# A two-layer hybrid network: one unused product in front of long runs of matrix products, and one loop turn written out on TensorE

## The chip, the cores and the metric

The kernel runs on one core of a Trainium2 chip (trn2). The metric is the time of one execution on the device, in microseconds (us). Every weight of the network comes from the chip's memory once; activations stay in the core's SBUF.

## The reference

One sequence of 256 tokens, width 1024, fp32, goes through two blocks.

```python
# first block: i = 0, 1
h = rms_norm(x, norm_mix_g[i])
x = x + (dsa_mixer(h, ...) if i == 0 else retention_mixer(h, ...))
x = x + conv_ffn(rms_norm(x, norm_ffn_g[i]), f_w_up[i], f_conv_w[i], f_conv_b[i], f_w_down[i])
# second block
h = rmsnorm(x, norm_mix_w) * (1 + scale_m) + shift_m
x = x + gate_m * hybrid_mixer(h, ...)
h = rmsnorm(x, norm_mlp_w) * (1 + scale_f) + shift_f
x = x + gate_f * (square(relu(h @ w_up)) @ w_down)
return rmsnorm(x, norm_final_w)
```

`dsa_mixer` is attention over a latent of 128 with an index that selects 64 keys; `retention_mixer` has 4 heads; `conv_ffn` projects 1024 to 2 x 2816, convolves over 3 tokens, gates by silu and projects back; `hybrid_mixer` joins a state-space scan (4 groups of 8 heads) and a pooling branch by gates. `c` enters by `silu(c) @ w_ada` as scale, shift and gate.

## The kernel before, in words

**Slabs.** All weights come as 381 slabs of 128 x 1024 fp32 (512 KB), in the order in which they are used, through a ring of six slots (`RING`). A slab holds eight 128x128 tiles. Numbers of the first slab of each stage are `S_AIN` (0), `S_AOUT`, `S_FFN0`, `S_B`, `S_BOUT`, `S_FFN1`, `S_DT`, `S_GRP`, `S_GATE`, `S_MERGE`, `S_WOUT`, `S_MLP`.

**The split multiplication.** TensorE multiplies in the format fp32r, and accuracy is kept by splitting both operands in two. ScalarE writes `w_hi` (L187, `split_hi`, a rounding copy), VectorE writes `w_lo = w_raw - w_hi` (L192, `split_lo`), and each tile then takes three products, `mm3`, lines L200 to L202: w_hi with the high part of the activation, w_hi with its low part, w_lo with its high part. The first operand of `pe.matmul` behind the output is the stationary one (128 weights columns), the second is the moving one, here 256 columns, the tokens. A profile row `ps<-a_hi,w_hi` is such a product; PEld rows are the loads of the stationary operand. `slab_gemm` does the eight tiles of one slab, 24 products, into one PSUM bank; `down_slab` uses one slab for eight output tiles, also 24 products; `two_slabs` takes two slabs tile by tile at the start of a stage, while the activation's tiles still arrive (`each(k)` waits for tile k). `both_slab` streams the high and low part of an activation as one moving operand of 512 columns (`L232`) with w_lo in another (`L233`).

**Operands in SBUF.** `w_raw`, `w_hi`, `w_lo` (6 x 4096 bytes per partition each) lie one behind the other, then a strip of 64 bytes, `between`, then `a_hi`, `a_lo`, `b_both` (tiles of 256 fp32, high and low), then `c_both`, whose tiles are 258 columns wide. So a tile of a_hi, a_lo or b_both begins 64 bytes past a multiple of 512 from any tile of weights, and the tiles of c_both begin at changing remainders.

**The order.** It is written out by hand for each engine and kept by semaphores: `w_lo_ready` counts split slabs (TensorE waits for it in `slab_ready`), `w_used` counts slabs that TensorE has finished, and frees the slot. TensorE goes through the stages `attention_pe`, `ffn_pe` (L = 0), `retention_pe`, `ffn_pe` (L = 1), `ssd_pe` and the last feed-forward.

- `ffn_pe` works on 22 pairs of up-slabs; the down-slab of pair p follows the up-slabs of pair p + 2. After the first pairs a hardware loop runs `LATER` = 4 turns of `UNROLL` = 4 pairs, on TensorE, ScalarE and VectorE alike; its semaphore values are computed from the turn (`val`). In the first feed-forward the slabs before the loop are 0 and 1 (two_slabs), 2 (`up_half(1, 0)`), a sum of squares, 3 (`up_half(1, 1)`), the pair 2 and `down(0)`; in the second they are `up_half(0, 0)`, a sum of squares (L264), `up_half(0, 1)` and so on.
- `retention_pe` has 12 slabs for each head j = 0 to 11, of which 4 to 7 (`v_slab`) have the activation as the stationary operand and 512 weights columns moving; `weigh` (L1246 to L1248) comes behind slab 8 and `sums` (L1252) behind slab 10. Head 0 is written out, heads 1 to 3 are a loop. `out_pe` is the output projection, m = 0 to 7, two slabs each here.
- `ssd_pe` works on four groups of 12 slabs (the small transposes L1588 and L1591 stand in it), `pools` (moving operand c_both), 16 gate slabs, the merge and `out_pe` with one slab for each m. Its `keep_going` is 24 unused products.

Row names in the profile: L1246 is a product of `weigh`, L1359 and L1374 are VectorE's lines in the retention heads (the decayed scores, and the low part of the heads' result, which is the operand of the output projection).

## Time and profile before

| | |
|---|---|
| median of three runs | 1194.18 us (1191.48 to 1194.28) |
| the profiled execution | 1193.18 us |
| its span, first to last instruction | 1191.4 us |
| mean granted TensorE clock | 0.998 |
| instructions | 25489, of them 9030 products on TensorE |
| busy: ScalarE | 712.9 us (60%) |
| bytes read from the chip's memory | 233.73 MB, 197 GB/s over the span |

The profile is one execution. Its page gives busy shares of the engines (PE is TensorE, DVE VectorE, ACT ScalarE), the chain of work that ended last, and groups of instructions by line. Products are pipelined: each is booked with its whole length, and the next starts before it ends, so the step between two products is not the length that a row shows. It has to be taken from starts: of single products in the timeline, or of the first and last product of a line in a stretch, with their number. "Idle" rows name what released an engine. Times in the timeline are microseconds from the span's start.

### The profile page before, as it was taken

To read this page: it belongs to the slowest core of one execution; us is meant where nothing else is said; L and a number is where in the kernel's file an instruction comes from. 1 tells how busy PE (TensorE), PEld (TensorE's weight loads), DVE (VectorE), ACT (ScalarE), POOL (GpSimd) and SP (SyncE) were. 2 spreads that over 40 slices of the span, in tenths; PEclk is the share of its full clock that TensorE was granted. 3 is DMA by queue.
4 is the path that set the end of the run, shared out by engine and by line. 5 is a ranking of instruction groups with operands and counts; after the bars stand their busy time and mean duration, and the time that the engine had idled before them with its cause. 6 is when DMAs were issued, how large, how long until landed. Compare 5 with 4: busy or idle time off the path is not lost.

```text
span 1191.4 us, 25489 instructions
## 1 busy us (share of the span) xinstructions
PE 1168.6 (98%) x9030; PEld 1114.1 (94%) x9030; DVE 976.2 (82%) x1775; ACT 712.9 (60%) x1111; POOL 33.3 (3%) x62
## 2 busy tenths in 40 slices
PE   9999999999999999999999999999999999999997
PEld 7989999999899999999999999999899899999996
DVE  7877998888998898899888799998996667666666
ACT  6577655556546456565555577877866456544553
POOL 0000000000000010000000000000000000000000
PEclk9999999999999999999999999999999999999999
DMA  7634676664766786756656436458545555655550
GB/s 279 188 114 165 207 238 227 223 221 151 242 235 229 265 295 230 251 193 232 224 198 192 161 112 244 148 188 184 169 159 196 187 185 211 200 189 186 184 176 36
DMA packets 72752, 235.71 MB, mean 198 GB/s; under 512 B 7392, under 2 KB 16096, under 8 KB 72560
## 3 DMA queue, kind: packets, MB, share of 16 engines
q1 hardware_dynamic: 64016, 203.86, 51.2%
q0 software_dynamic: 8528, 30.98, 7.6%
q8 instruction: 41, 0.67, 0.2%
q14 instruction: 23, 0.19, 0.1%
q10 hardware_dynamic: 144, 0.02, 0.0%
HBM read 233.73 MB, written 1.09 MB: 197 GB/s over the span
## 4 chain that ended last, share of the span: by engine, by line
PE 83%; DVE 9%; ACT 4%; issue 3%; DMA 0%; DVEq 0%; SPq 0%; ACTq 0%
PE ps L200 25%; PE ps L201 24%; PE ps L202 24%; PE ps L232 3%; DVE w_lo L192 3%; PE ps L233 2%; DVE arena L1937 1%; ACT w_hi L187 1%; PE ps L1602 1%; DMA w_raw<-stream 0%; ACT arena L756 0%; DVE arena L1925 0%; DVE arena L453 0%; PE ps L1236 0%; PE ps L1246 0%
## 5 line engine op out<-in xcount | busy, mean ns | idle before, releaser
L200 PE MATMUL ps<-a_hi,w_hi 128*128 128x256 f32 x1656 | 468.0, 283 | 2.4 <-DVE w_lo L192 1.6
L192 DVE TENSOR_TENSOR w_lo<-w_raw,w_hi 128x1024 fp32r<-128x1024 f32 x381 | 461.1, 1218 | 10.6 <-ACT w_hi L187 4.8
L201 PE MATMUL ps<-a_lo,w_hi 128*128 128x256 f32 x1656 | 462.2, 279 | 0.0
L202 PE MATMUL ps<-a_hi,w_lo 128*128 128x256 f32 x1656 | 461.9, 279 | 0.0
L187 ACT ACTIVATE w_hi<-w_raw 128x1024 fp32r<-128x1024 f32 x381 | 390.6, 1048 | 23.3 <-PE ps L202 17.9
L200 PEld LDWEIGHTS ps<-a_hi,w_hi 128*128 128x128 f32 x1656 | 310.9, 188 | 7.9 <-issue 3.8
L201 PEld LDWEIGHTS ps<-a_lo,w_hi 128*128 128x128 f32 x1656 | 310.6, 188 | 0.5
L202 PEld LDWEIGHTS ps<-a_hi,w_lo 128*128 128x128 f32 x1656 | 310.7, 188 | 0.2 <-issue 0.2
L200 PE MATMUL ps<-b_both,w_hi 128*128 128x256 f32 x560 | 158.1, 282 | 4.2 <-DVE b_both L927 3.5
L201 PE MATMUL ps<-b_both,w_hi 128*128 128x256 f32 x560 | 156.4, 279 | 0.0
L202 PE MATMUL ps<-b_both,w_lo 128*128 128x256 f32 x560 | 156.3, 279 | 0.0
L200 PEld LDWEIGHTS ps<-b_both,w_hi 128*128 128x128 f32 x560 | 105.1, 188 | 6.4 <-DVE b_both L927 4.7
L201 PEld LDWEIGHTS ps<-b_both,w_hi 128*128 128x128 f32 x560 | 105.1, 188 | 0.0
L202 PEld LDWEIGHTS ps<-b_both,w_lo 128*128 128x128 f32 x560 | 105.0, 188 | 0.0
L1026 ACT ACTIVATE arena<-arena,par 128x256 f32<-128x256 f32 x88 | 52.7, 601 | 74.5 <-DVE arena L1087 74.5
L201 PE MATMUL ps<-c_both,w_hi 128*128 128x258 f32 (+1 forms) x280 | 79.5, 284 | 0.0
L200 PE MATMUL ps<-c_both,w_hi 128*128 128x258 f32 (+1 forms) x280 | 79.0, 282 | 0.0
L202 PE MATMUL ps<-c_both,w_lo 128*128 128x258 f32 (+1 forms) x280 | 78.8, 281 | 0.0
L2171 ACT ACTIVATE arena<-arena 128x256 f32<-128x256 f32 x32 | 16.4, 512 | 82.8 <-DVE arena L2222 82.8
L1037 ACT ACTIVATE b_both<-arena 128x256 fp32r<-128x256 f32 x44 | 18.4, 419 | 71.8 <-DVE arena L1101 71.8
L453 DVE CUSTOM_DVE_ANT_0 arena<-arena 128x1024 f32<-128x1024 f32 x48 | 58.5, 1219 | 1.3 <-DMA arena<-ada 1.1
L1087 DVE TENSOR_TENSOR arena<-ps,inv 128x256 f32<-128x256 f32 x88 | 36.9, 421 | 23.6 <-PE ps L202 23.5
(309 smaller groups left out, 1665.5 us busy)
## 6 DMA issues: line engine op xcount, KB each, us to landing
w_raw<-stream SPq DMA_DIRECT2D x381, 512.0 KB, 3.8
arena<-ada POOLq DMA_DIRECT2D x48, 512.0 KB, 5.3
c_both<-cum_rows POOLq DMA_DIRECT2D x4, 1024.0 KB
arena<-x SPq DMA_DIRECT2D x2, 512.0 KB, 4.5
con<-consts SPq DMA_DIRECT2D x1, 1024.0 KB, 5.8
arena<-row_cols POOLq DMA_DIRECT2D x2, 512.0 KB
out<-arena SPq DMA_DIRECT2D x4, 256.0 KB, 2.2
arena<-c_rows POOLq DMA_DIRECT2D x1, 512.0 KB, 4.2
```

The source lines that it names most:

```text
L187: act.activation(w_hi[:, s % RING], w_raw[:, s % RING], ACT.Copy).then_inc(w_hi_ready, 1)
L192: dve.tensor_tensor(w_lo[:, s % RING], w_raw[:, s % RING], w_hi[:, s % RING].bitcast(F32), ALU.subtract).then_inc(w_lo_ready, 1)
L200: pe.matmul(o, wh, xh, start=start, stop=False, skip_group_check=shared)
L201: pe.matmul(o, wh, xl, start=False, stop=False, skip_group_check=shared)
L202: return pe.matmul(o, wl, xh, start=False, stop=stop, skip_group_check=shared)
L232: pe.matmul(ps[:, bank, :].rearrange("p (i t) -> p i t", i=2), w_hi[:, s % RING, t], both[:, k], start=first and k == 0, stop=False)
L233: mm = pe.matmul(ps[:, bank, 0:SEQ], w_lo[:, s % RING, t], both[:, k, 0], start=False, stop=last and k == NT - 1)
L453: dve.tensor_tensor_reduce(ada_raw[:, DOT_BUF[i]], ada_raw[:, DOT_BUF[i]], cond_row, 1.0, 0.0, ALU.mult, ALU.add, o).then_inc(dot_done, 1)
L1026: act.activation(conv[:, p % 2, half], up[:, p % 2, half], ACT.Identity, bias=prm(p, 6 + half, it), scale=prm(p, 3 * half + 2, it)).then_i ...
L1037: act.activation(b_hi[:, p % 4], glu[:, p % 2], ACT.Copy).then_inc(f["hi"], 1)
L1087: dve.tensor_tensor(up[:, p % 2, half], ps[:, 6 - 2 * (p % 2) + half, 0:SEQ], inv[:, :], ALU.mult).then_inc(f["up_out"], 1)
L2171: act.activation(relu[:, n % 3], up_m[:, n % 3], ACT.Relu, bias=up_shift[:, n % 3:n % 3 + 1]).then_inc(relu_ready, 1)
```

## The change

A new helper, `settle`, issues one product at the beginning of a run: stationary operand the first tile of w_hi in the ring slot of the coming slab, moving operand the first 256 columns of w_lo in the same slot, into the PSUM bank that the run is about to fill. Its result is not used, since the first real product of the run starts the accumulation anew. The two operands lie exactly `RING * SLAB` elements (24576 bytes) apart, the "zero distance" of the change's name: both begin at the same remainder of 4096. `slab_gemm`, `two_slabs` and the helpers above them get a flag `lead` that asks for it, behind the wait for the slab and, where tiles are awaited one by one, behind the wait for the first tile. It is set for attention slabs 0 and 4; in the first feed-forward for the two first slabs, slab 3 and the first slab of the loop's first turn; in each retention head for slabs 9 and 11, and for the two first slabs of head 0; in the second feed-forward for its second slab; for gate slab 3; and in both `out_pe` for m = 1.

So that the loop of the first feed-forward has it once and not in each turn, its first turn is written out in front of it on TensorE, and its loop there starts at turn 1. The other engines' programs are unchanged.

```diff
--- before.py
+++ after.py
@@ -201,22 +201,32 @@
             pe.matmul(o, wh, xl, start=False, stop=False, skip_group_check=shared)
             return pe.matmul(o, wl, xh, start=False, stop=stop, skip_group_check=shared)
 
-        def slab_gemm(pe, s, o, hi, lo, it=None, ds=0, first=True, last=True, each=None):
+        def settle(pe, s, o):
+
+            pe.matmul(o, w_hi[:, s % RING, 0:P], w_lo[:, s % RING, 0:SEQ], start=True, stop=True)
+
+        def slab_gemm(pe, s, o, hi, lo, it=None, ds=0, first=True, last=True, each=None, lead=False):
 
             slab_ready(pe, s, it, ds)
+            if lead and each is None:
+                settle(pe, s, o)
             for k in range(NT):
                 if each:
                     each(k)
+                    if lead and k == 0:
+                        settle(pe, s, o)
                 t = slice(k * P, (k + 1) * P)
                 mm = mm3(pe, o, w_hi[:, s % RING, t], w_lo[:, s % RING, t], hi[:, k], lo[:, k],
                          first and k == 0, last and k == NT - 1)
             mm.then_inc(w_used, 1)
 
-        def two_slabs(pe, s, outs, hi, lo, each):
+        def two_slabs(pe, s, outs, hi, lo, each, lead=False):
 
             slab_ready(pe, s + 1)
             for k in range(NT):
                 each(k)
+                if lead and k == 0:
+                    settle(pe, s, outs[0])
                 t = slice(k * P, (k + 1) * P)
                 for i, o in enumerate(outs):
                     n = (s + i) % RING
@@ -401,10 +411,10 @@
                     pe.wait_ge(taken, base + m - 3)
                 o = ps[:, 4 + (m + 2) % 4, 0:SEQ]
                 if two:
-                    slab_gemm(pe, s0 + 2 * m, o, hi, lo, last=False, each=None if m else each[0])
+                    slab_gemm(pe, s0 + 2 * m, o, hi, lo, last=False, each=None if m else each[0], lead=m == 1)
                     slab_gemm(pe, s0 + 2 * m + 1, o, hi[:, NT:2 * NT], lo[:, NT:2 * NT], first=False, each=None if m else each[1])
                 else:
-                    slab_gemm(pe, s0 + m, o, hi, lo, each=None if m else each[0])
+                    slab_gemm(pe, s0 + m, o, hi, lo, each=None if m else each[0], lead=m == 1)
 
         def out_act(act, s0, per, v, g):
             load_root_table(act, v)
@@ -524,8 +534,8 @@
             def operand(k):
                 pe.wait_ge(a_ready, k + 1)
 
-            def in_slab(n, each=None):
-                slab_gemm(pe, n, ps[:, in_bank(n), 0:SEQ], a_hi, a_lo, each=each)
+            def in_slab(n, each=None, lead=False):
+                slab_gemm(pe, n, ps[:, in_bank(n), 0:SEQ], a_hi, a_lo, each=each, lead=lead)
 
             def key_sums(n):
                 pe.wait_ge(key_sq, n + 1)
@@ -569,7 +579,7 @@
                                    ki_dup[r, 0:w], start=True, stop=True)
                 mm.then_inc(idx_ready, 1)
 
-            in_slab(0, operand)
+            in_slab(0, operand, lead=True)
             in_slab(1)
             in_slab(2)
             in_slab(3)
@@ -578,7 +588,7 @@
             pe.wait_ge(res_ready, NT)
             key_sums(0)
             key_sums(1)
-            in_slab(4)
+            in_slab(4, lead=True)
             in_slab(5)
             pe.wait_ge(key_diag, 1)
             pe.matmul(ps[:, 7, :], ones, diag[:, :, :].rearrange("p b t -> p (b t)"), start=True, stop=True).then_inc(key_spread, 1)
@@ -974,16 +984,16 @@
 
         def ffn_pe(pe, L, s0, v):
 
-            def up_half(p, half, it=None, each=None):
+            def up_half(p, half, it=None, each=None, lead=False):
 
                 if p >= 2:
                     pe.wait_ge(f["up_out"], val(2 * FF_PAIRS * L + 2 * (p - 2) + half + 1, it, 2 * UNROLL))
-                slab_gemm(pe, pair_at(s0, p) + half, ps[:, 6 - 2 * (p % 2) + half, 0:SEQ], a_hi, a_lo, it, 3 * UNROLL, each=each)
-
-            def up_pair(p, it=None):
+                slab_gemm(pe, pair_at(s0, p) + half, ps[:, 6 - 2 * (p % 2) + half, 0:SEQ], a_hi, a_lo, it, 3 * UNROLL, each=each, lead=lead)
+
+            def up_pair(p, it=None, lead=False):
 
                 for half in range(2):
-                    up_half(p, half, it)
+                    up_half(p, half, it, lead=lead and not half)
 
             def down(p, it=None):
                 pe.wait_ge(f["operand"], val(FF_PAIRS * L + p + 1, it, UNROLL))
@@ -992,17 +1002,21 @@
             if L:
                 up_half(0, 0, each=ready(a_ready, NT * v)(pe))
                 sum_added(pe, v)
-                up_half(0, 1)
+                up_half(0, 1, lead=True)
                 up_half(1, 0)
             else:
-                two_slabs(pe, s0, [ps[:, 6 + half, 0:SEQ] for half in range(2)], a_hi, a_lo, ready(a_ready, NT * v)(pe))
+                two_slabs(pe, s0, [ps[:, 6 + half, 0:SEQ] for half in range(2)], a_hi, a_lo, ready(a_ready, NT * v)(pe), lead=True)
                 up_half(1, 0)
                 sum_added(pe, v)
-            up_half(1, 1)
+            up_half(1, 1, lead=not L)
             pe.wait_ge(inv_ready, v)
             up_pair(2)
             down(0)
-            with pe.Fori(0, LATER) as it:
+            if not L:
+                for u in range(UNROLL):
+                    up_pair(3 + u, lead=u == 0)
+                    down(1 + u)
+            with pe.Fori(0 if L else 1, LATER) as it:
                 for u in range(UNROLL):
                     up_pair(3 + u, it)
                     down(1 + u, it)
@@ -1261,9 +1275,9 @@
                     if 4 <= j < 8:
                         v_slab(own, j - 4, it)
                     elif h == 0 and j == 0:
-                        two_slabs(pe, own, [ps[:, i, 0:SEQ] for i in range(2)], a_hi, a_lo, ready(a_ready, 2 * NT)(pe))
+                        two_slabs(pe, own, [ps[:, i, 0:SEQ] for i in range(2)], a_hi, a_lo, ready(a_ready, 2 * NT)(pe), lead=True)
                     elif h or j > 1:
-                        slab_gemm(pe, own, ps[:, j % 4, 0:SEQ], a_hi, a_lo, it, HEAD)
+                        slab_gemm(pe, own, ps[:, j % 4, 0:SEQ], a_hi, a_lo, it, HEAD, lead=j in (9, 11))
                     if h == 0 and j == 2:
                         sum_added(pe, 2)
                     if h == 0 and j == 3:
@@ -1660,7 +1674,7 @@
                     pe.wait_ge(u_done, 2 * GROUPS)
                 else:
                     pe.wait_ge(gate_ready, m - 3)
-                slab_gemm(pe, gate_at(m), ps[:, m % 4, 0:SEQ], a_hi, a_lo)
+                slab_gemm(pe, gate_at(m), ps[:, m % 4, 0:SEQ], a_hi, a_lo, lead=m == 3)
                 if m == 2:
                     tail_sums(GROUPS - 1, None)
 
```

TensorE in the first feed-forward, from the last product of `down(0)` into the loop, before (names as in the profile: output, then operands; L200 to L202 are the split multiplication, `ISA` and branch rows belong to the loop, `ffn_up_out` counts VectorE's evictions of the up-slabs):

```order
L202 MATMUL ps<-b_both,w_lo 128x256
L1005 UNCONDITIONAL_BRANCH
L1005 ISA
L196 ISA [waits ffn_up_out]
L200 MATMUL ps<-a_hi,w_hi 128x256 [waits w_lo_ready]
L201 MATMUL ps<-a_lo,w_hi 128x256
L202 MATMUL ps<-a_hi,w_lo 128x256
```

The same place after, where the written-out turn now begins,

```order
L202 MATMUL ps<-b_both,w_lo 128x256
L206 MATMUL ps<-w_lo,w_hi 128x256 [waits w_lo_ready,ffn_up_out]
L200 MATMUL ps<-a_hi,w_hi 128x256
L201 MATMUL ps<-a_lo,w_hi 128x256
L202 MATMUL ps<-a_hi,w_lo 128x256
```

and the entrance of its loop, one turn later:

```order
L202 MATMUL ps<-b_both,w_lo 128x256
L1019 UNCONDITIONAL_BRANCH
L1019 ISA
L196 ISA [waits ffn_up_out]
L200 MATMUL ps<-a_hi,w_hi 128x256 [waits w_lo_ready]
```

What moved: the lead (L206) now carries the two waits of the turn's first slab, and the entrance of the loop, with its branch, stands 12 slabs (288 products) further back.

TensorE in the second feed-forward, from the last product of `up_half(0, 0)` over the sum of squares (L264) to `up_half(0, 1)`, before:

```order
L202 MATMUL ps<-a_hi,w_lo 128x256
L264 MATMUL ps<-sq,con 128x256 [waits sq_added]
L200 MATMUL ps<-a_hi,w_hi 128x256 [waits w_lo_ready]
L201 MATMUL ps<-a_lo,w_hi 128x256
L202 MATMUL ps<-a_hi,w_lo 128x256
```

and after, where the sum is at L274:

```order
L202 MATMUL ps<-a_hi,w_lo 128x256
L274 MATMUL ps<-sq,con 128x256 [waits sq_added]
L206 MATMUL ps<-w_lo,w_hi 128x256 [waits w_lo_ready]
L200 MATMUL ps<-a_hi,w_hi 128x256
L201 MATMUL ps<-a_lo,w_hi 128x256
L202 MATMUL ps<-a_hi,w_lo 128x256
```

What moved: one product stands between the sum and the slab, and has taken over the wait for w_lo; nothing else in this feed-forward differs.

## Rows read from the trace of the kernel before

**Rows 1.** The page's first part: busy time and share of the span.
```profile
PE 1168.6 (98%) x9030; PEld 1114.1 (94%) x9030; DVE 976.2 (82%) x1775; ACT 712.9 (60%) x1111; POOL 33.3 (3%) x62
```

**Rows 2.** The page's chain that ended last, by line.
```profile
PE ps L200 25%; PE ps L201 24%; PE ps L202 24%; PE ps L232 3%; DVE w_lo L192 3%; PE ps L233 2%; DVE arena L1937 1%; ACT w_hi L187 1%; PE ps L1602 1%; DMA w_raw<-stream 0%; ACT arena L756 0%; DVE arena L1925 0%; DVE arena L453 0%; PE ps L1236 0%; PE ps L1246 0%
```

**Rows 3.** Line L202: count, min/median/max ns, first and last start, in three stretches.
```profile
L202 PE MATMUL ps<-a_hi,w_lo x343: 279/279/279, 498.8 to 673.3; 128*128 128x256 f32 x172
L202 PE MATMUL ps<-b_both,w_lo x176: 279/279/279, 512.6 to 681.8; 128*128 128x256 f32 x176
...
L202 PE MATMUL ps<-a_hi,w_lo x304: 279/279/279, 125.8 to 283.8; 128*128 128x256 f32 x152
L202 PE MATMUL ps<-b_both,w_lo x166: 279/279/279, 131.5 to 291.6; 128*128 128x256 f32 x166
...
L202 PE MATMUL ps<-b_both,w_lo x113: 278/280/280, 455.3 to 494.8; 128*128 128x256 f32 x113
```

**Rows 4.** The same view of L202 in three other stretches.
```profile
L202 PE MATMUL ps<-a_hi,w_lo x31: 276/276/276, 43.4 to 53.6; 128*128 128x256 f32 x31
...
L202 PE MATMUL ps<-a_hi,w_lo x23: 276/276/276, 104.8 to 112.3; 128*128 128x256 f32 x23
...
L202 PE MATMUL ps<-a_hi,w_lo x32: 276/276/276, 898.8 to 909.3; 128*128 128x256 f32 x32
```

**Rows 5.** Timeline of TensorE (start, length) at three starts, and L202 behind two.
```profile
125.50 0.39 PE L200 MATMUL ps<-a_hi,w_hi 128*128 128x256 f32 x1 [0.82 <-DVE w_lo L192]
125.73 0.28 PE L201 MATMUL ps<-a_lo,w_hi 128*128 128x256 f32 x1
...
757.73 0.37 PE L200 MATMUL ps<-a_hi,w_hi 128*128 128x256 f32 x1
757.93 0.28 PE L201 MATMUL ps<-a_lo,w_hi 128*128 128x256 f32 x1
...
L202 PE MATMUL ps<-a_hi,w_lo x17: 276/276/276, 758.0 to 763.5; 128*128 128x256 f32 x17
...
717.97 0.36 PE L200 MATMUL ps<-a_hi,w_hi 128*128 128x256 f32 x1
718.17 0.28 PE L201 MATMUL ps<-a_lo,w_hi 128*128 128x256 f32 x1
...
L202 PE MATMUL ps<-a_hi,w_lo x16: 279/279/279, 718.3 to 723.6; 128*128 128x256 f32 x16
```

**Rows 6.** Timeline of TensorE in the pool projection, moving operand c_both.
```profile
895.94 0.29 PE L202 MATMUL ps<-c_both,w_lo 128*128 128x256 f32 x1
896.07 0.28 PE L200 MATMUL ps<-c_both,w_hi 128*128 128x256 f32 x1
896.18 0.29 PE L201 MATMUL ps<-c_both,w_hi 128*128 128x256 f32 x1
896.31 0.29 PE L202 MATMUL ps<-c_both,w_lo 128*128 128x256 f32 x1
```

**Rows 7.** Timeline of VectorE and TensorE around three slabs of the first feed-forward.
```profile
124.23 1.22 DVE L192 TENSOR_TENSOR w_lo<-w_raw,w_hi 128x1024 fp32r<-128x1024 f32 x1
...
132.56 1.22 DVE L192 TENSOR_TENSOR w_lo<-w_raw,w_hi 128x1024 fp32r<-128x1024 f32 x1
...
134.09 0.28 PE L200 MATMUL ps<-a_hi,w_hi 128*128 128x256 f32 x1
```

**Rows 8.** Waits of TensorE from 300 to 455 us: total, times, longest.
```profile
PE ps L1246 <- DVE arena L1359: 0.7, 1, 0.7
PE ps L200 <- DVE b_both L1374: 0.7, 2, 0.5
```

**Rows 9.** Windows: length, busy us of PE, PEld, DVE, ACT, POOL, clock, DMA.
```profile
44.00:53.00 9.00, 9.00 (x81) 9.00 (x81) 8.75 (x33) 5.40 (x10) 0.00 (x0) 1.00 0.52 154
...
140.00:180.00 40.00, 40.00 (x342) 40.00 (x341) 37.25 (x63) 25.42 (x38) 1.59 (x3) 1.00 0.71 233
```

**Rows 10.** The page's costliest groups: VectorE's split of a slab.
```profile
L192 DVE TENSOR_TENSOR w_lo<-w_raw,w_hi 128x1024 fp32r<-128x1024 f32 x381 | 461.1, 1218 | 10.6 <-ACT w_hi L187 4.8
```

## Prediction

> **What bounds the kernel now.** I read the page first. TensorE is busy in 98% of the span, VectorE in 82% [rows 1], and in the chain that ended last lines L200 to L202, the three products of the split multiplication, hold 73% [rows 2]. So time is made of products multiplied by the step from one product to the next. "Busy" says nothing of that step, because a product is booked with 279 ns while the next one starts long before it ends. I therefore asked for line L202 in long stretches: the row gives the number of its products and the start of the first and the last one, and there is one L202 product in every three.
>
> In the second feed-forward 343 + 176 = 519 of them start between 498.8 and 681.8 us [rows 3]: 183.0 us over 518 steps is 353.3 ns for three products, **117.8 ns for one**. In the first feed-forward's loop 304 + 166 = 470 start between 125.8 and 291.6 us: 353.5 ns, again 117.8; the output projection of the retention (113 from 455.3 to 494.8 us) gives 352.7. But there are runs of the same instruction and shapes, at the same granted clock of 1.00, the 2.4 GHz level [rows 9], that go faster: 31 from 43.4 to 53.6 us, 340 ns for three; 23 from 104.8 to 112.3 us, 341; 32 from 898.8 to 909.3 us, 339 [rows 4]. That is **113.3 ns for one**. The booked time differs too, 276 against 279 or 280 ns, so a row shows at a glance which pace its stretch had. Within a stretch minimum, median and maximum are equal or nearly so: a run keeps the pace it began with, across slabs, across the loop's turns and from a_hi to b_both as moving operand. The pace is a property of how the run started.
>
> What decides it the rows don't tell outright. Two runs behind the very same code, the two small transposes of L1591 in two groups of the state-space part, have the same 0.20 us between their first two products; one then goes on with products of 276 ns, the other with 279 [rows 5]. After the wait that ends at 125.50 us (first to second product 125.73 - 125.50 = 0.23 us) the long loop began slow and stayed slow for all its slabs. Where the moving operand's place relative to the weights' changes from product to product (the tiles of c_both lie 258 columns apart, those of a_hi 256), the step wanders: 0.13, 0.11, 0.13 us in a row [rows 6], and right behind it stands the 113 ns stretch of 898.8 us. So the relative place of the two operands acts on the step, and a run can be pushed from one pace into the other. That is what the change tries: one product whose two operands lie a whole number of slabs apart, w_lo against w_hi of the same ring slot, put at the start of a run.
>
> **The change, part by part.** (1) Leads: 14 places, two of them in the loop over heads that turns three times, so 12 + 6 = 18 executed. Each is one 128x256 product; I cost it at one step, 0.118 us: 18 x 0.118 = 2.1 us on the path, since TensorE is the path nearly everywhere. Bounds: nothing, where it stands in a gap that ends with another engine's work; 0.23 us, the first step after a wait [rows 5]: 4.1 us for all. I take the 2.1, nearest to the rows of running products.
>
> (2) The runs behind them, in slabs of 24 products. First feed-forward from the unrolled turn on: 59 slabs. Second, from its second slab: 65. Output projection of the retention from its third slab: 14. Heads: slabs 9 and 10 four times, 8; slab 11 with the next head's first four, 3 x 5, and the last slab 11: 16. Attention slabs 4 and 5: 2. Gates 3 to 11: 9. Output of the state-space part, tiles 1 to 7: 7. Together 180 slabs, 4320 products. If each goes from 117.8 to 113.3 ns that is 4320 x 4.5 ns = **19.4 us**. Bounds of this term: nothing (no run changes pace) and the full 4.5 ns; below nothing if the lead pushes a run to a slower step (third rival). I take the full 4.5, because only two steady paces occur on this pair of operands, a run holds what it has, and a product at another distance is the one thing that I see precede a change of pace.
>
> (3) Runs that bring nothing. Up-slab 3, pair 2 and the first down-slab of the first feed-forward (113 us on) end in a wait for VectorE's w_lo, which ended at 125.45 us (124.23 + 1.22) [rows 7]: whatever TensorE saves there it waits longer; zero. The first four slabs of the attention could give 96 x 4.5 = 0.4 us; their successors are short sums that also wait for others; zero, with 0.4 kept for the range. The two places with two slabs at once are fast already.
>
> (4) The retention heads. From the heads to the output projection TensorE waits for two results of VectorE, three times, 1.4 us together [rows 8], and a faster TensorE asks for them earlier. Of the gain on the heads' 24 slabs, 24 x 24 x 4.5 ns = 2.6 us, I take off 1.0. Their 512-column products step otherwise and I count nothing for them.
>
> (5) Unrolling the first turn on TensorE: 288 more products are written out, none more is executed, and the loop starts at turn 1 for the first feed-forward. The semaphore values are the same. The output projection at 455 us is written out too and has the loop's pace [rows 3], so I cost this at zero; the cover would be gone if the instruction stream were not there in time, which would show as a gap at the loop's entrance.
>
> (6) What a faster TensorE runs into. A slab takes 24 x 113.3 = 2.72 us instead of 2.83; three slabs 8.16 instead of 8.48. VectorE is busy 37.25 of 40 us in the loop's first turns [rows 9]; for the same work it would need 93% x 8.48 = 7.90 of 8.16 us, 97%. It still keeps up, barely. The closest point is the fourth slab of the loop: its w_lo is ready at 132.56 + 1.22 = 133.78 us and TensorE takes it up at 134.09 [rows 7], 0.31 us later. Three slabs at the fast pace reach it 3 x 24 x 4.5 = 0.32 us sooner, the lead puts 0.12 back: 0.11 us of slack are left. One split of a slab takes 1218 ns [rows 10] and cannot be later by chance by much; but this is the thinnest point of the sum.
>
> The sum: 19.4 - 2.1 - 1.0 = 16.3 us off the profiled execution, which took 1193.2 us (span 1191.4): **1176.9, say 1177 us**. The median of the three runs shown, 1194.2, lies 1 us above that execution, within their own spread.
>
> A rule of the skill speaks against all this. The trace has two paces for the same product and a wandering one where the operands' distance changes [rows 3, 4, 6]. The Trainium skill, page "TensorE: Matmul & The Clock Gate", section on what happens when you issue a matmul, says that TensorE reads the moving operand and the next weights through two independent ports, so that loading the next tile's weights steals no read bandwidth from the running product. By that rule no distance matters, the second term of the sum is zero and 2.1 us of leads remain. The rows of this trace disagree with it as far as a common step goes, and the sum follows the rows.
>
> **Rivals.** *First, only part of the runs change.* For it: the slack of 0.11 us at the loop's fourth slab, since behind the wait that ends at 125.50 us the pace was the slow one. If a short stall there throws the run back, 56 of the 59 slabs stay slow: 56 x 24 x 4.5 = 6.0 us less, about 1183 us. The same price holds if the lead works at some places only. *Second, the change does not do what it says*: the pace is drawn by chance at each start and the lead has no say (for it: [rows 5], same code, both outcomes). Then 2.1 us are added: 1195.3 us. A chance draw could still favour one long run, which would be the first rival again. The page's rule gives this same time. *Third, the other side: the lead sets a slower pace.* The steps on c_both are 0.12 us in the mean [rows 6]; a run held at 120 ns costs 4320 x 2.2 ns = 9.5 us and the leads 2.1: 1204.8 us. It decides from a small point on: since 3.6 us are 0.3%, it takes 1.5 us over 4320 products, 0.35 ns each; losing today's 113 ns stretches (about 500 products, 2.2 us, seven stretches, three of them in [rows 4]) would suffice as well: 1197.5 us. Against it: on a_hi and b_both no steady run slower than 117.8 ns stands in the trace.
>
> **How the numbers follow.** Forecast 0.57, first rival 0.15, second 0.13, third 0.15. I take 0.3% (3.6 us) as the least that a measurement can tell from no change: faster 0.57 + 0.15 = 0.72, same 0.13, slower 0.15. The forecast's own range: at best the leads cost nothing (2.1), nothing is absorbed in the heads (1.0), the first slabs count (0.4), and some short runs that begin anew get 113 ns as well, 500 products or 2.2 us: 1171.2. At worst the leads cost 4.1 and all of the heads' gain is absorbed: 1176.9 + 2.0 + 1.6 = 1180.5. The range for all has to take in the first and the second rival and leaves out the third, 0.15, and a little at the lower end: 1171.5 to 1195.5 us.
>
> **What would show it.** Right: L202 in the two feed-forwards at 276 ns instead of 279, 519 starts in 176 us instead of 183; the loop of the first from lead to end 6.4 us shorter; L206 x18. First rival: 276 ns up to some gap near 134 us, 279 behind it. Second: 279 ns in both loops and only L206 added. Third: more than 279 ns, or today's 276 ns stretches gone. The forecast is wrong if the feed-forwards stay at 353 ns for three products, or if they go at 340 ns and the span falls by less than 10 us, since a new wait must then have taken the rest.

## The result, and the profile after

The change took 1195.37 us (median of ten executions, 1192.99 to 1197.12) against 1191.63 us for the kernel before (also ten): a ratio of 1.0022, 95% interval 1.0014 to 1.0031. The ratio stands for 2.6 us more (the two medians are 3.7 apart), within the 0.3% that I had called no change; since its interval leaves out 1, the change made the kernel a little slower, where I had forecast 16 us less. 1177.0 us was forecast; the time is at the upper edge of the range, and it is the second rival's, "the change does not do what it says", 1195.3 us. All ratios in this text leave out one execution of the kernel before, 1264.61 us at a mean granted clock of 0.849 instead of 0.995 or more.

The profiled execution took 1195.14 us, its span 1193.4, two more than before. The page's first part and its chain, which answer to [rows 1, 2]:

```profile
PE 1172.4 (98%) x9048; PEld 1117.9 (94%) x9048; DVE 976.2 (82%) x1775; ACT 713.1 (60%) x1111; POOL 33.2 (3%) x62
PE ps L200 24%; PE ps L202 24%; PE ps L201 24%; PE ps L242 3%; DVE w_lo L192 3%; DVE arena L1951 2%; PE ps L243 2%; ACT w_hi L187 1%; DVE arena L1939 1%; DVE arena L1933 1%; ACT arena L766 0%; PE ps L578 0%; DVE arena L463 0%; PE ps L1250 0%; PE ps L1616 0%
```

9048 products are 9030 and the 18 leads. The chain is what it was. The answer is in line L202 (number of products, min/median/max ns, first and last start), first feed-forward, then second:

```profile
L202 PE MATMUL ps<-a_hi,w_lo x295: 279/279/279, 128.0 to 282.8; 128*128 128x256 f32 x148
L202 PE MATMUL ps<-b_both,w_lo x144: 279/279/279, 133.7 to 280.3; 128*128 128x256 f32 x144
...
L202 PE MATMUL ps<-a_hi,w_lo x328: 279/279/279, 506.5 to 675.8; 128*128 128x256 f32 x164
L202 PE MATMUL ps<-b_both,w_lo x152: 279/279/279, 516.1 to 671.2; 128*128 128x256 f32 x152
```

439 products from 128.0 to 282.8 us are 154.8 us over 438 steps, 353.4 ns for three; 480 from 506.5 to 675.8 are 353.4 too. That is 117.8 ns a product, as in [rows 3]: the leads stand there and the pace behind them did not move. Here is one of them (timeline of TensorE, start and length), right behind the wait for w_lo of [rows 5, 7]:

```profile
127.61 0.35 PE L206 MATMUL ps<-w_lo,w_hi 128*128 128x256 f32 x1 [0.80 <-DVE w_lo L192]
127.81 0.28 PE L200 MATMUL ps<-a_hi,w_hi 128*128 128x256 f32 x1
127.93 0.28 PE L201 MATMUL ps<-a_lo,w_hi 128*128 128x256 f32 x1
128.05 0.28 PE L202 MATMUL ps<-a_hi,w_lo 128*128 128x256 f32 x1
```

Even a 113.3 ns stretch of before was gone. The 23 products of [rows 4] from 104.8 to 112.3 us had 276 ns; in the change they have 279:

```profile
L202 PE MATMUL ps<-a_hi,w_lo x23: 279/279/279, 106.9 to 114.7; 128*128 128x256 f32 x23
```

Two differences between the profiles have nothing to do with leads. From 32 to 37 us the granted clock (the column behind PE's busy time and count) fell in the profile after, to 0.53 in the second window, near the 1.2 GHz level. TensorE was busy without a gap before and during the fall, in both kernels, and the DMA share (the next column) was near 1 in both. First the change, then the kernel before:

```profile
32.00:34.00 2.00, 2.00 (x14) 0.85 0.99 387
34.00:37.00 3.00, 3.00 (x16) 0.53 1.01 352
```
```profile
32.00:34.00 2.00, 2.00 (x18) 1.00 1.03 427
34.00:37.00 3.00, 3.00 (x27) 1.00 1.06 350
```

16 products instead of 27 fall in those 3 us. When each product's start is compared with that of the same product before, the change gets 1.5 us later in this place. In the other direction go the waits of the state-space part (700 to 850 us: total, times, longest). Change, then before:

```profile
PE ps L1605 <- ACT arena L1732: 1.4, 3, 0.6
PE ps L1616 <- DVE arena L1939: 0.6, 2, 0.3
PE ps L1587 <- DVE arena L1885: 0.4, 1, 0.4
```
```profile
PE ps L1591 <- ACT arena L1718: 2.4, 3, 1.8
PE ps L1602 <- DVE arena L1925: 1.0, 2, 0.5
PE ps L1573 <- DVE arena L1871: 0.4, 1, 0.4
```

3.8 us became 2.4. It is no work of the change either. The 1.8 us, a wait at 840 us, is an exception of the one execution profiled before: in the other twelve kernels profiled for this text no wait of this line is longer than 0.6 us, and three of them have the code of the kernel before up to its last product. One of these (the table, below):

```profile
PE ps L1591 <- ACT arena L1718: 1.1, 3, 0.6
```

Product by product, the 2.0 us between the spans come together like this: 18 leads at 0.118 are 2.1 us, the clock 1.5, a lost 113.3 ns stretch (71 products at 107 us) 0.3; at 840 us the change wins back 1.6, and about 0.3 in small waits. A second stretch, at 295 us, also fell to 117.8 ns, but what it lost was won back within 9 us. Among the shorter stretches of the state-space part some are fast in one profile and some in the other; in all, 432 products stand in stretches of 20 and more at 113.3 ns, against 482 before.

### The profile page after: what moved, and what is told of

It is laid out like the page before. It is cut to its first block, busy times and chain, and to the rows that moved or that the text cites. A ratio compares the mean times of both kernels' runs of the same rounds, so it can differ in the third digit from the quotient of the medians.

```text
span 1193.4 us, 25511 instructions
## 1 busy us (share of the span) xinstructions
PE 1172.4 (98%) x9048; PEld 1117.9 (94%) x9048; DVE 976.2 (82%) x1775; ACT 713.1 (60%) x1111; POOL 33.2 (3%) x62
## 4 chain that ended last, share of the span: by engine, by line
PE 81%; DVE 11%; issue 4%; ACT 3%; DVEq 1%; ACTq 0%
PE ps L200 24%; PE ps L202 24%; PE ps L201 24%; PE ps L242 3%; DVE w_lo L192 3%; DVE arena L1951 2%; PE ps L243 2%; ACT w_hi L187 1%; DVE arena L1939 1%; DVE arena L1933 1%; ACT arena L766 0%; PE ps L578 0%; DVE arena L463 0%; PE ps L1250 0%; PE ps L1616 0%
## 5 line engine op out<-in xcount | busy, mean ns | idle before, releaser
L200 PE MATMUL ps<-a_hi,w_hi 128*128 128x256 f32 x1656 | 466.6, 282 | 0.7 <-DVE a_lo L1456 0.7
L202 PE MATMUL ps<-a_hi,w_lo 128*128 128x256 f32 x1656 | 462.2, 279 | 0.0
L200 PEld LDWEIGHTS ps<-a_hi,w_hi 128*128 128x128 f32 x1656 | 311.1, 188 | 5.1 <-issue 4.1
L202 PEld LDWEIGHTS ps<-a_hi,w_lo 128*128 128x128 f32 x1656 | 311.4, 188 | 0.0
L200 PE MATMUL ps<-b_both,w_hi 128*128 128x256 f32 x560 | 158.3, 283 | 4.1 <-DVE b_both L937 3.5
L202 PE MATMUL ps<-b_both,w_lo 128*128 128x256 f32 x560 | 156.2, 279 | 0.0
L200 PEld LDWEIGHTS ps<-b_both,w_hi 128*128 128x128 f32 x560 | 105.2, 188 | 6.4 <-DVE b_both L937 4.7
L202 PEld LDWEIGHTS ps<-b_both,w_lo 128*128 128x128 f32 x560 | 105.1, 188 | 0.0
L200 PE MATMUL ps<-c_both,w_hi 128*128 128x258 f32 (+1 forms) x280 | 79.0, 282 | 0.0
L202 PE MATMUL ps<-c_both,w_lo 128*128 128x258 f32 (+1 forms) x280 | 78.8, 282 | 0.0
```

Of the source, the lines that this page charges most:

```text
L200: pe.matmul(o, wh, xh, start=start, stop=False, skip_group_check=shared)
L202: return pe.matmul(o, wl, xh, start=False, stop=stop, skip_group_check=shared)
```

## First round: which part of the change does what

Two theories at this point. **Chance**: the pace of a run is drawn at its start and no lead has a say. **Distance**: the place of the moving operand relative to the weights decides, and the change put it in the wrong place.

**Only the unrolled turn** (no leads):
```diff
-            if lead and each is None:
-                settle(pe, s, o)
...
-                    if lead and k == 0:
-                        settle(pe, s, o)
```


> The change without its leads: only the first loop turn of the first feed-forward is written out on TensorE. Theory A (the leads do it all: 18 products of about 0.12 us on the path, and runs that they hold at 117.8 ns): ratio 1.000, within 0.3 us of before, both two-slab stretches at 276 ns per product as before, no gap at the entrance of the loop. Theory B (writing the turn out costs something, in the instruction stream or at the loop's entrance): 0.5 us or more over before, with a gap on TensorE near 125 or 159 us.

Measured: 1192.84 us, ratio 0.9998 (0.9989 to 1.0008). The unrolled turn costs nothing that shows, 1 us at most. Its stretches at 107 and 295 us went at 117.8 ns without any lead in front, so their loss in the change is no proof against the leads:

```profile
L202 PE MATMUL ps<-a_hi,w_lo x23: 278/280/280, 106.9 to 114.7; 128*128 128x256 f32 x23
```

The kernel before gave one execution of 1184.16 us among the 29 measured beside these three kernels. 8 us is about what one long run at 113.3 ns would bring with some short ones; no profile shows that execution.

**Only the leads** (the loop whole again, and so 17 of them):
```diff
-            if not L:
-                for u in range(UNROLL):
-                    up_pair(3 + u, lead=u == 0)
-                    down(1 + u)
-            with pe.Fori(0 if L else 1, LATER) as it:
+            with pe.Fori(0, LATER) as it:
```


> The 17 leads without the written-out turn (so none in front of the loop). Theory A: ratio 1.001 to 1.002 as for the whole change, 2.0 us of leads less those that stand in a wait, and 0.6 us for the two stretches of 71 products that fall from 113.3 to 117.8 ns. Where the granted clock falls near 34 us of the span, 1.5 us more in that execution. Theory B: within 0.5 us of before.

Measured: 1194.65 us, ratio 1.0015 (1.0005 to 1.0025), 1.8 us (0.6 to 3.0) for 17 leads, or 0.11 each if nothing else is in it; both feed-forwards at 117.8 ns. Within these intervals the leads make up the whole loss.

**The leads at the run's own distance**, 64 bytes past a multiple of 256, instead of at zero:
```diff
-            pe.matmul(o, w_hi[:, s % RING, 0:P], w_lo[:, s % RING, 0:SEQ], start=True, stop=True)
+            pe.matmul(o, w_hi[:, s % RING, 0:P], hi[:, 0], start=True, stop=True)
```


> The whole change, but the lead's moving operand is the first tile of the run's own activation (64 bytes past, the distance of all products behind it) and not w_lo. Theory A1 (a product at zero distance holds the run at 117.8 ns, one at 64 bytes says nothing): the two-slab stretches near 106 and 294 us are back at 276 ns, the other led runs stay at 279 or get 276 in one of six, time 0.5 us below the change. Theory A2 (the distance has no say, the pace is drawn by the exact moment of the start): about one led run in seven at 276 ns, wherever it is, and the time that of the change within 0.5 us plus what a long run's draw gives (6 to 7 us less if a feed-forward is among them).

Measured: 1194.64 us, ratio 1.0020 (1.0004 to 1.0036), long runs at 117.8 ns; one of the two stretches with two slabs at once went at 113.4 (295.9 us), the other at 117.8. Such a lead is one product more and nothing else. For time, zero distance and the run's own can't be told apart. It takes a probe that looks at many distances.

## Second round: distance and phase

**A sweep of distances** behind the last product of the kernel before: 64 leads from 0 to 504 bytes past zero distance, 12 ordinary products behind each, and the same again behind an fp32 product. The probe's products are thrown away. `at(d)` issues a lead at d bytes, `products(4)` four tiles, so twelve ordinary products. The moving operand of these leads is a piece of b_both, the stationary one always the same tile of w_hi.
```diff
+            for d in range(0, 512, 8):
+                at(d)
+                products(4)
+            for d in range(0, 512, 8):
+                pe.matmul(ps[:, 7, 0:SEQ], ones, const("cos", SEQ), start=True, stop=True)
+                at(d)
+                products(4)
```


> Before, with unused products behind the last one: first, without any break, for each distance of 0, 8, 16 to 504 bytes one product at that distance and 12 ordinary ones at 64 bytes (four tiles of a slab against a_hi and a_lo); then the same with an fp32 product of 256 columns in front of each. About 205 us more than before. Theory A1: the 12 products behind distance 0 step at 117.8 ns in both parts, and there are other distances (the tiles of c_both reach 176 and 184 bytes in front of the 113 ns stretch of before) behind which they step at 113.3. Theory A2: the step does not change inside the first part at all, whatever the distance; in the second part it changes with no order by distance.

Measured, from starts: within the run 113.3 ns follows on leads at 24, 72 and 160 bytes, and again at 280, 328 and 416; behind the fp32 product at 16, 168 and 200, and again at 272, 424 and 456. Nowhere else. The list repeats after 256 bytes, which chance does not do; and it is another list when the run begins in another way, which distance alone does not do.

**A table**: a lead at zero distance, 12, 13 or 14 ordinary products, a lead at distance d, 12 ordinary products; then (fourth part, not shown in the cut of code) zero, 12, a lead at 24, 12, d, 9. `ordinary(n)` issues n ordinary products.
```diff
+            for extra in range(3):
+                for d in range(0, 256, 8):
+                    at(0)
+                    ordinary(12 + extra)
+                    at(d)
+                    ordinary(12)
```


> Before, with 3700 unused products behind the last one, about 435 us more. Each case begins with a lead at zero distance and 12, 13 or 14 ordinary products (64 bytes), then one product at 0, 8, 16 to 248 bytes, then 12 ordinary ones; a fourth part does the same from a 113 ns stretch made by a product at 24 bytes. In the sweep before this one 24, 72 and 160 bytes (and each of them plus 256) were followed by 113.3 ns, all others by 117.8. Theory C (the step is a function of a small hidden phase of TensorE and of the distance: the 117.8 ns pace goes through three phases in turn, the 113.3 ns pace has one): the result depends on the distance and on the number of products ahead, modulo three, and on nothing else; 24 bytes behind 12 products gives 113.3 in all 32 cases of the fourth part; zero distance gives 117.8 from each phase. Theory D (the pace depends on the moment, and the three distances were luck): the 32 cases with 24 bytes in the fourth part differ among themselves, about one in ten at 113.3.

Measured: 113.3 ns follows on 24, 32, 56, 152, 160 with 12 products between, on 8, 24, 224 with 13, on 8, 24, 144, 160, 216, 224 with 14; on zero never. The change of pace looks like this (timeline; L2169 is the lead at 24 bytes, L2179 an ordinary product):

```profile
1207.08 0.28 PE L2179 MATMUL ps<-a_lo,w_hi 128*128 128x256 f32 x1
1207.19 0.28 PE L2179 MATMUL ps<-a_hi,w_lo 128*128 128x256 f32 x1
1207.31 0.28 PE L2169 MATMUL ps<-b_both,w_hi 128*128 128x256 f32 x1
1207.43 0.28 PE L2179 MATMUL ps<-a_hi,w_hi 128*128 128x256 f32 x1
...
1208.34 0.28 PE L2179 MATMUL ps<-a_hi,w_lo 128*128 128x256 f32 x1
1208.45 0.28 PE L2179 MATMUL ps<-a_hi,w_hi 128*128 128x256 f32 x1
```

1207.43 to 1208.45 us are nine steps of 113.3 ns; nine steps before the lead, from 1206.25 to 1207.31, take 1.06 us. In the fourth part a lead at 24 made 113.3 ns in 20 cases of 32, and that with the same 13 products in front each time. So something decides that the order of the products does not hold.

It is the phase. I folded the trace's starts, which are given to the nanosecond, by a period, and looked for the one at which the starts of 113.3 ns stretches coincide. At **6.6667 ns** they do, over whole traces. 113.3 ns is 17 such periods: these products all start at one phase. At 117.8 ns three steps are 53 periods, and the starts go round three phases, measured at 0.25, 0.87 and 0.50 of the period, counted from the place of the 113.3 ns products; I call them 2, 7 and 4 (eighths). A lead moves the run from phase to phase. In both probes 352 leads stand behind a run of ordinary products, and 341 of them had a readable state before and behind them (the phase that the lead's place would have had; "113" for the other pace). They fall in 102 pairs of distance and phase, 52 of them seen more than once, and **none of these has two outcomes**. The two lines of the table that are used below:

```
lead at     from 2       from 7       from 4       from 113
 0 bytes    4 (34x)      2 (48x)      2 (34x)      4 (17x)
24 bytes    2 (12x)      113 (23x)    113 (2x)     2 (1x)
```

This is **Theory C**: the pace hangs on distance modulo 256 bytes and on the phase at the lead, in a fixed way. It says why the change failed: zero distance leads to the 117.8 ns pace from everywhere, from 113 too. The change's own profile agrees, since the products behind each of its 18 leads go at 117.8 ns. And it says what would work. A lead at zero distance leaves phase 4 or 2. Ordinary products turn 2 to 7, 7 to 4, 4 to 2, so after a number of steps with remainder 2 by three the two are 7 and 4, and 24 bytes send both to 113 (from 4 in only two cases so far).

One thing no run here separates. All tiles of weights begin at the same remainder of 256, so "distance to the weights" and "place of the moving operand in SBUF, modulo 256 bytes" go together, in every probe and in every kernel. I go on saying distance; which of the two acts is not shown.

## Third round: the word

I call a lead at zero distance, a number of ordinary products and a lead at 24 bytes, taken together, the word.

**The pair of leads by itself**, behind 96 different beginnings (32 distances, 12 to 14 products), with 13 ordinary products between the two, and again with 1:
```diff
+            for between in (13, 1):
+                for n in range(96):
+                    at(n * 8 % 256)
+                    ordinary(12 + n // 32)
+                    at(0)
+                    ordinary(between)
+                    at(24)
+                    ordinary(12)
```


> The kernel before with unused products behind its last one: 192 times a lead at one of 32 distances (it sets a starting phase), 12, 13 or 14 ordinary products, then a lead at zero distance, n ordinary products, a lead at 24 bytes and 12 ordinary products. n is 13 in the first 96 cases and 1 in the last 96. Theory C: the 12 products behind the lead at 24 bytes go at 113.3 ns in all of the first 96, whatever was before; in the last 96 too if the phases are settled after one product, which the table does not show. Chance theory: in about one of seven.

Measured: with 13 between, 113.3 ns in **96 cases of 96**, though only 9 of them had it before the pair; with 1 between, in none of 96. Two steps lie between the leads here, remainder 2 as well, so the remainder is not enough. I read it like this: one product does not bring the run back to its round of phases, and the table holds only for a run that is in it. Ordinary products behind the lead at zero, behind the lead at 24, and behind the pair with one between:

```profile
L2179 PE MATMUL ps<-a_hi,w_lo x5: 280/280/280, 1186.4 to 1188.0; 128*128 128x256 f32 x5
...
L2179 PE MATMUL ps<-a_lo,w_hi x4: 276/276/276, 1188.4 to 1189.5; 128*128 128x256 f32 x4
...
L2179 PE MATMUL ps<-a_lo,w_hi x4: 280/280/280, 1645.8 to 1646.9; 128*128 128x256 f32 x4
```

**The word in the kernel**: the change without its leads, and in three long runs a lead at zero distance in front of one slab, an ordinary product and a lead at 24 bytes in front of a later one, 26 or 50 products on.
```diff
+            if word == 1:
+                at(pe, s, o, 0)
+            if word == 2:
+                pe.matmul(o, w_hi[:, s % RING, 0:P], hi[:, 0], start=True, stop=True)
+                at(pe, s, o, 24)
...
-                    up_pair(3 + u, lead=u == 0)
+                    up_pair(3 + u, word=u == 2)
```


> The change with other leads in other places: none of its 18, but two leads per long run, placed once the run is steady. The first at zero distance, the second 26 products later with its moving operand 24 bytes further than zero distance, an ordinary product thrown away between them: three extra products per run, in three runs (first feed-forward from the loop's third pair, second from its second pair, output projection of the retention from its third tile). Theory C (each product starts at a fixed phase of a steady 6.67 ns period, the 117.8 ns pace is a cycle of three phases, the 113.3 ns pace one phase, and a lead maps phase to phase in a fixed way; worked out from the table of distances: the lead at zero distance leaves two of the three phases, 26 steps later they are the two that a lead at 24 bytes sends to 113.3 ns): the three runs go at 113.3 ns from the second lead to their end, in every execution; 55 x 24, 63 x 24 and 10 x 24 products, 3072 x 4.5 ns = 13.8 us less 9 x 0.117 = 1.1 us: about 1179 us, ratio 0.989. Chance theory (the pace is drawn at each start, leads don't decide): 117.8 ns in nearly all, about 1193 us. If VectorE cannot follow, the first run falls back at a stall and the gain is 6 us less: about 1185 us.

Measured: **1180.89 us** (1177.54 to 1181.14), ratio 0.9898 (0.9879 to 0.9918), 11.5 us less than the 1192.36 of before. L202 in the two feed-forwards:

```profile
L202 PE MATMUL ps<-a_hi,w_lo x263: 275/276/277, 148.3 to 280.9; 128*128 128x256 f32 x132
L202 PE MATMUL ps<-b_both,w_lo x134: 275/276/277, 150.6 to 282.9; 128*128 128x256 f32 x134
...
L202 PE MATMUL ps<-a_hi,w_lo x310: 275/277/277, 506.7 to 663.4; 128*128 128x256 f32 x155
L202 PE MATMUL ps<-b_both,w_lo x176: 276/276/277, 508.7 to 671.6; 128*128 128x256 f32 x176
```

486 products in the last two rows from 506.7 to 671.6 us are 340.0 ns for three, 113.3 for one, to the end of the run. The first feed-forward holds 113.3 ns through all turns of the loop: VectorE follows.

**The same with 88 bytes for 24**:
```diff
-                at(pe, s, o, 24)
+                at(pe, s, o, 88)
```


> The same kernel, three extra products per run at the same places, but the second lead stands at 88 bytes instead of 24. Theory C: the table has no phase that a lead at 88 bytes sends to 113.3 ns, so all three long runs stay at 117.8 ns from the lead on: 9 x 0.117 = 1.1 us added to before, 1193 us, ratio 1.001. A theory in which any lead, or their place alone, does it expects the same time as for 24 bytes.

Measured: 1193.22 us, ratio 1.0008 (0.9996 to 1.0020). The same number of products in the same places, all runs at 117.8 ns. The 12.3 us between the two kernels come from the 64 bytes by which the second lead's operand is moved.

```profile
L202 PE MATMUL ps<-a_hi,w_lo x327: 280/280/280, 506.8 to 675.7; 128*128 128x256 f32 x164
L202 PE MATMUL ps<-b_both,w_lo x152: 280/280/280, 515.3 to 670.4; 128*128 128x256 f32 x152
```

**Without the product between**, so that 25 steps lie between the leads in the feed-forwards (49 in the output projection):
```diff
             if word == 2:
-                pe.matmul(o, w_hi[:, s % RING, 0:P], hi[:, 0], start=True, stop=True)
                 at(pe, s, o, 24)
```


> The kernel with leads at zero and 24 bytes at the three long runs, without the ordinary product between them, so that the second lead comes 25 products behind the first, not 26. Theory C: now it hangs on the phase before the first lead. Of the three phases of the 117.8 ns pace (2, 4 and 7 eighths of the 6.67 ns period) a lead at zero distance in the place of phase 4 or 7 leaves phase 2, which after 25 steps is phase 7, and 24 bytes make 113.3 ns of it; in the place of phase 2 it leaves phase 4, which becomes 2, and the run stays at 117.8 ns. So each long run has the pace that the phase of its first lead says, which the trace shows: two in three at 113.3 ns. A theory in which the two leads suffice expects all three at 113.3 ns.

Measured: 1187.20 us in one execution. Two of three runs at 113.3 ns, and each as its phase says: the first feed-forward was at the 113.3 ns pace when its lead at zero came, which leaves 4, then 2 after 25 steps, so 117.8 ns; the output projection and the second feed-forward had phase 7, which leaves 2, then 7, so 113.3. The output projection behind its second lead, and the second feed-forward:

```profile
L202 PE MATMUL ps<-b_both,w_lo x80: 276/277/277, 470.6 to 497.5; 128*128 128x256 f32 x80
...
L202 PE MATMUL ps<-a_hi,w_lo x328: 275/276/277, 506.9 to 669.7; 128*128 128x256 f32 x164
```

This profile also shows what I had reckoned with in step (6). Its first feed-forward happened to begin at 113.3 ns (129.31 us), and at the loop's fourth slab TensorE had to wait for VectorE's split, which ended at 136.28 + 1.22 = 137.50 us:

```profile
136.28 1.22 DVE L192 TENSOR_TENSOR w_lo<-w_raw,w_hi 128x1024 fp32r<-128x1024 f32 x1
...
137.32 0.28 PE L201 MATMUL ps<-b_both,w_hi 128*128 128x256 f32 x1
137.44 0.28 PE L202 MATMUL ps<-b_both,w_lo 128*128 128x256 f32 x1
137.65 0.36 PE L200 MATMUL ps<-a_hi,w_hi 128*128 128x256 f32 x1
137.84 0.28 PE L201 MATMUL ps<-a_lo,w_hi 128*128 128x256 f32 x1
```

Two steps of 0.21 and 0.19 instead of 0.11 us: 0.18 us lost. The run went on at 113.3 ns behind it, so a stall does not always change the pace.

**The word earlier, and in a fourth run**: from the loop's first pair on, its lead at zero the first product behind the wait for w_lo, and in the gates.
```diff
-                    up_pair(3 + u, word=u == 2)
+                    up_pair(3 + u, word=u == 0)
...
+                slab_gemm(pe, gate_at(m), ps[:, m % 4, 0:SEQ], a_hi, a_lo, word={4: 1, 5: 2}.get(m, 0))
```


> The kernel with leads at zero and 24 bytes and the product between them, moved forward in the first feed-forward to the loop's first pair, and added to a fourth run, the gates (fourth and fifth gate behind the first). Theory C: all four runs at 113.3 ns. Six more slabs in the first feed-forward, 0.65 us, seven in the gates, 0.75 less 0.35 us: about 1 us less than with the word at the third pair. Step (6) of the prediction says that VectorE then still keeps up by 0.1 us at the fourth slab; if it does not, the first feed-forward has a gap near 135 us and stays at 117.8 ns behind it: about 5.5 us more than with the word at the third pair.

Measured: 1183.14 us, ratio 0.9910 (0.9888 to 0.9932), a miss. The six executions stand in two groups, 1178.22, 1180.57, 1181.05 and 1185.22, 1185.23, 1186.35. The profiled one is the last: the gates and the other two at 113.3 ns, the first feed-forward at 117.8, without the gap near 135 us that the expectation named for that case.

```profile
127.28 0.36 PE L206 MATMUL ps<-w_lo,w_hi 128*128 128x256 f32 x1 [0.92 <-DVE w_lo L192]
127.48 0.28 PE L200 MATMUL ps<-a_hi,w_hi 128*128 128x256 f32 x1
...
L202 PE MATMUL ps<-a_hi,w_lo x253: 279/281/281, 148.4 to 282.7; 128*128 128x256 f32 x127
```

The lead behind the wait left phase 7 (the starts behind it stand at 0.90 of the period), which a lead at zero distance never leaves in a steady run; 26 steps on that is phase 2, from which 24 bytes lead to 2. So I put the first lead where the run is steady.

**The first lead 24 products behind the wait**:
```diff
-                    up_pair(3 + u, word=u == 0)
+                    up_pair(3 + u, word={0: (0, 1), 1: (2, 0)}.get(u))
```


> As the kernel with the word in four runs, but in the first feed-forward the lead at zero distance stands at the loop's second slab, 24 products behind the wait for VectorE, not directly behind it, and the product and the lead at 24 bytes at the fourth slab, 50 products later (50 and 26 leave the same remainder by three). Theory C: in all executions all four runs go at 113.3 ns; against the word at the third pair four slabs more in the first feed-forward (0.4 us) and 0.4 us in the gates: about 1180 us, ratio 0.989, and no execution near 1185 us, as half of them were with the lead directly behind the wait. If VectorE cannot follow from the fourth slab on, a gap in the first feed-forward and about 1185 us in some of them.

Measured: 1180.95 us, ratio 0.9908 (0.9894 to 0.9921), five executions from 1179.24 to 1182.52 and none near 1185. All four runs at 113.3 ns. The word as it stands in the first feed-forward (L214 the ordinary product, L206 the lead at 24 bytes), and L202 behind it:

```profile
136.67 0.28 PE L214 MATMUL ps<-a_hi,w_hi 128*128 128x256 f32 x1
136.78 0.28 PE L206 MATMUL ps<-w_lo,w_hi 128*128 128x256 f32 x1
136.90 0.28 PE L200 MATMUL ps<-a_hi,w_hi 128*128 128x256 f32 x1
...
L202 PE MATMUL ps<-a_hi,w_lo x263: 276/276/276, 148.4 to 281.0; 128*128 128x256 f32 x132
```

The 0.8 us that I expected from the earlier place and the gates over the word in three runs do not show in the medians (1180.95 and 1180.89); they are within the spread.

## Why the prediction was wrong

By its own steps:

- *What bounds the kernel*: right. What TensorE's step saves reaches the kernel's time almost whole. The word took 4.5 ns off each of about 3020 products, 13.6 us, and put 9 products in, 1.1 us; that leaves 12.5, and the ratio of 0.9898 stands for 12.2 (the medians are 11.5 apart).
- *Step (1)*, 2.1 us for 18 leads: right. 1.8 us for 17 with the leads alone; the nine products of the 88-byte kernel cost 0.9 us at a ratio of 1.0008, with an interval that holds zero.
- *Step (2)*, 19.4 us for 4320 products: **this step failed**; it measured nothing. Its reason was that "only two steady paces occur", that a run holds its pace, and that "a product at another distance is the one thing that I see precede a change of pace". The first two are so. The third is not the whole of it: the kernel with the unrolled turn alone had its stretches at 107 and 295 us at another pace with no such product in front. And from all three together it does not follow that this distance leads to the better pace. From [rows 6] I took that distance acts and assumed the direction. In the change both feed-forwards stayed at 353.4 ns for three products, and zero distance goes to 117.8 ns in all 133 cases of the two probes whose state in front and behind can be read.
- *Step (3)*, *step (4)*: not put to the test by the change, since no run behind a lead became faster. The 113.3 ns stretches that I counted as safe were drawn anew in each execution: the kernel with the unrolled turn alone lost them without a lead.
- *Step (5)*, unrolling at zero: right as far as it can be measured, 0.9998.
- *Step (6)*, the thin point at the loop's fourth slab: right in place and nearly in size. 0.31 us less three slabs' 0.32 is nothing left without a lead; measured were 0.18 us lost there. Behind that place VectorE keeps up: with the word, 113.3 ns held to the end.
- *The rivals*: the second came true in its time. In part that is luck: the leads cost what it says, but its 1195.3 starts from the profiled 1193.2 and not from the median of 1191.63, and its mechanism, that the lead has no say, is refuted. A lead within a steady run decides the pace behind it, by its distance and the phase. The third was half right in its mechanism, since zero distance sends a run to the slower of the two paces; but none went slower than 117.8 ns, and one lost stretch of 0.3 us is far from its 1197.5 or 1204.8. Of the first nothing came: no led run changed to the faster pace. The rule of the Trainium skill that I set against the change (page "TensorE: Matmul & The Clock Gate", what happens when you issue a matmul: two independent ports) gives 1195.3 us as well, and the measured 1195.37 seems to bear it out. What I drew from it, that the operand's place has no effect on the step, is contradicted by the kernels with 24 and with 88 bytes, 12.3 us apart. What the page itself says, that the load of weights takes nothing from the running product, no run here tests, since the weights' remainder never changed. A right time is no proof of the reason.
- *The chances*: 0.13 for what happened was too little. [rows 5] showed one code with two outcomes; a change that sets one product in front of it had to be put at more than that as long as nothing in the trace showed its own distance followed by the 113.3 ns pace.

## What to carry to other kernels

A back-to-back run of the same product can have two paces, and the length in a row (276 or 279 ns) tells which; compare starts, not lengths, to price it. When a trace shows that something acts, ask it for the direction too, and if it can't say, sweep that quantity in a probe behind the kernel before building on one value: one execution each of two such probes settled what three timed kernels could not. Three thrown-away products per long run, the first at a steady place, brought 1% here. The distances and remainders are measured for this product alone (fp32r, 128 rows, 256 columns, weights in tiles of 512 bytes); any other needs its own table.

## What the runs showed that I had not expected

- The starts of TensorE's products keep to a period of 6.6667 ns through a whole execution, 17 periods for a step at the 113.3 ns pace and 53 for three steps at the other. What hardware has this period, and why distance counts by 256 bytes, no run here shows; it stays open.
- Short falls of the granted clock come and go by themselves. From 28 to 44 us the mean was 0.89 in 6 of the 13 kernels profiled, and 1.00 in the other 7, with early leads (the change) and without (the unrolled turn alone, and the sweep, whose code is the kernel before up to its last product). Each such fall is worth the 1.5 us above. A second place is near 57 us: there it fell in 8 of the 13, among them the kernel with the leads alone, where the mean from 57 to 59 us was 0.54. In the profiles of the kernel before and of the table it fell in neither. The executions of the kernel before sort by it: 20 with a mean clock of 0.998 have a median of 1191.3 us, 13 with 0.995 one of 1194.7. So most of the spread in this text goes with this clock, and a difference of 2 us wants executions of equal clock beside each other. Those exist: at 0.997 the change has 1194.9 (4 executions) against 1192.5 (19, measured beside the later kernels), at 0.996 it has 1196.0 (5) against 1193.2 (11).
- The first product behind a wait can stand at a phase outside the three (in the profile of the word moved forward the first three are at 0.40, 0.35 and 0.05 of the period). The word begun right behind the wait worked, by their times, in half of six executions; begun 24 products later in all five, and at the loop's third pair in all five. These are few executions, and why it fails where it fails was read in one profile.
